# Four expert picks per tile moved out of the choice of experts and into the two output slots of the second layer

## The reference

```python
def second_block(x, c, ...):
    for layer in range(DEPTH):                        # 2 layers
        h = modulate(rmsnorm(x, ...), sh1, sc1)
        y = mlstm_mixer(h, ...) if layer < 1 else stick_breaking_mixer(h, k_sh, v_sh, ...)
        x = x + g1[:, None, :] * y                    # the output product ends in w_out
        h = modulate(rmsnorm(x, ...), sh2, sc2)
        x = x + g2[:, None, :] * peer_ffn(h, ...)

def peer_ffn(h, w_q, sub_keys, peer_u, peer_v):       # per block of 128 tokens
        q = einsum('td,de->te', xb, w_q)              # 8 heads
        s = einsum('thpk,pnk->thpn', q, sub_keys)
        s_top, i_top = lax.top_k(s, 16)
        ...                                           # 16 of 256 pairs -> expert numbers, softmax g
        u = jnp.take(peer_u, expert, axis=0)
        act = gelu(einsum('thkd,td->thk', u, xb))
        vv = jnp.take(peer_v, expert, axis=0)
        return einsum('thk,thkd->td', g * act, vv)
```

## Time and profile before

| | |
|---|---|
| Median of 3 runs | 2549.08 us (2549.06 to 2549.9) |
| Profiled execution | span 2555.0 us; no other time of it is given |
| PE busy | 81% of the span |
| DVE busy | 67% |
| DMA share, while experts are gathered | 0.9 or more in 21 of the last 22 slices |
| Gathers (software_dynamic queue) | 57.4% of 16 engines' span |

### The profile page before, as it was taken

How to read it: one execution, slowest core, us unless ns; L and a number is a source line. 1 busy time by engine, 2 the same in 40 slices (tenths; PEclk the granted TensorE clock), 3 DMA queues, 4 the chain that set the end, 5 groups by cost and what they waited for, 6 DMA issues and landing times.

```text
span 2555.0 us, 33871 instructions
## 1 busy us (share of the span) xinstructions
PE 2064.9 (81%) x12150; PEld 1390.3 (54%) x12150; DVE 1720.0 (67%) x3454; ACT 953.7 (37%) x2101; POOL 652.0 (26%) x631
## 2 busy tenths in 40 slices
PE   8999999999999999997755587795587787555555
PEld 7999898899989979874211132261133344111111
DVE  5687777768777767575985556538956745955444
ACT  4444443454444345432332225322325623222222
POOL 0000001000000100033454433324433424344443
PEclk9999999999999999998877798797798889677777
DMA  7545577664547754379999999999999989999998
GB/s 300 212 168 202 200 272 282 245 246 167 205 180 266 288 203 165 135 280 378 411 417 419 422 419 422 409 415 421 421 419 418 421 360 363 390 407 421 422 421 355
DMA packets 110515, 828.17 MB, mean 324 GB/s; under 512 B 14384, under 2 KB 15296, under 8 KB 30992
## 3 DMA queue, kind: packets, MB, share of 16 engines
q0 software_dynamic: 90000, 595.97, 57.4%
q1 hardware_dynamic: 20352, 230.08, 23.5%
HBM read 824.95 MB, written 1.05 MB: 323 GB/s over the span
## 4 chain that ended last, share of the span: by engine, by line
PE 48%; DMA 22%; DVE 16%; ACT 5%; issue 4%; DVEq 2%; POOL 1%; ACTq 1%; PEldq 0%; SPq 0%; POOLq 0%; PEld 0%
PE pd L600 14%; PE pa L600 11%; DMA ring_b<-in_peer_uv,eidx 10%; PE pr L1225 9%; DMA wring<-in_peer_uv,eidx 7%; PE pr L600 5%; DMA ring_c<-in_peer_uv,eidx 3%; DVE wring L2588 2%; DVE ring_b L2588 2%; PE pa L1246 2%; PE pa L1340 2%; DVE wring_r L1887 2%; PE pd L1246 1%; DMA aring<-in_ada_rows 1%; DMA wring<-in_w_mix 1%
## 5 line engine op out<-in xcount | busy, mean ns | idle before, releaser
L1225 PE MATMUL pr<-ring_b,junk 128*64 128x512 f32 x928 | 391.0, 789 | 171.2 <-ACT junk L1653 166.5
L1225 PE MATMUL pr<-wring,junk 128*64 128x512 f32 x888 | 366.4, 781 | 174.4 <-ACT junk L1653 172.2
L1831 POOL DMA_INDIRECT ring_b<-in_peer_uv,eidx x232 | 272.0, 1173 | 605.1 <-PE pr L1225 377.7
L2588 DVE CUSTOM_DVE_ANT_0 ring_b<-ring_b,hrow 128x1024 f32<-128x1024 f32 x232 | 282.9, 1225 | 211.0 <-DMA ring_b<-in_peer_uv,eidx 201.7
L2588 DVE CUSTOM_DVE_ANT_0 wring<-wring,hrow 128x1024 f32<-128x1024 f32 x222 | 270.2, 1224 | 189.5 <-DMA wring<-in_peer_uv,eidx 184.5
L1831 POOL DMA_INDIRECT wring<-in_peer_uv,eidx x222 | 251.0, 1131 | 317.9 <-PE pr L1225 271.5
L1643 ACT ACTIVATE gel<-dots 128x2 f32<-128x2 f32 x255 | 51.8, 203 | 699.5 <-DVE dots L2588 697.5
L1225 PEld LDWEIGHTS pr<-ring_b,junk 128*64 128x64 f32 x928 | 90.3, 167 | 392.4 <-ACT junk L1653 264.6
L1225 PEld LDWEIGHTS pr<-wring,junk 128*64 128x64 f32 x888 | 83.8, 164 | 385.0 <-ACT junk L1653 277.4
L1817 POOL DMA_DIRECT2D aring<-in_ada_rows x112 | 60.2, 538 | 841.7 <-DVE adal L1982 841.5
L1887 DVE TENSOR_TENSOR wring_r<-wring,wtop 128x2048 fp32r<-128x2048 f32 x76 | 171.8, 2262 | 56.4 <-ACT wtop L1370 54.2
(11 more groups left out here) (417 smaller groups left out, 4484.0 us busy)
## 6 DMA issues: line engine op xcount, KB each, us to landing
wring<-in_w_mix SPq DMA_DIRECT2D x38, 2048.0 KB, 8.5
aring<-in_ada_rows POOLq DMA_DIRECT2D x112, 512.0 KB, 5.2
wring<-in_w_stick SPq DMA_DIRECT2D x24, 2048.0 KB
wring<-in_w_ffn SPq DMA_DIRECT2D x22, 2048.0 KB, 8.3
wring<-in_w_lstm SPq DMA_DIRECT2D x12, 2048.0 KB, 7.7
wring<-in_w_back SPq DMA_DIRECT2D x8, 2048.0 KB, 8.2
wring<-in_w_back SPq DMA_DIRECT2D x4, 1536.0 KB, 7.2
ring_b<-in_peer_uv,eidx POOLq DMA_INDIRECT x232
```

What stands on the lines that cost most here:

```text
L1225: m = nc.tensor.matmul(pr[half][side, :], diag[:, p % DIAGS, :], row(p)[:, D + half * 512:D + (half + 1) * 512], start=p in FIRST_OF_SIDE, ...
L1831: pool.indirect_dma_start(out=row(q), out_offset=None, in_=ins["peer_uv"], in_offset=bass.IndirectOffsetOnAxis(ap=eidx[:, tt % NT, CHOSEN[ ...
L2588: m = nc.vector.tensor_tensor_reduce(out=row(q)[:, 0:D], in0=row(q)[:, 0:D], in1=hrow[:, q // PICKS % NT, SIDE[q], :], scale=1.0, scalar=0 ...
```

## The change

The plan gets a new entry, "mid", of four picks between "o" and the first output slot. The picks of the choice go from 41 to 37 for block 0 and from 31 to 27 for block 1. PE serves picks in the middle of each output slot (after four of its eight products): up to "mid" - 2 in slot 6 and up to "mid" in slot 7. DVE serves picks up to "mid" instead of "o" ahead of the first output product. ACT's calls read the same table; its next call after "o" already reaches past "mid". All picks from there to the end of the choice come four places earlier.

```diff
-    out, q, step = ((3, 3, 41), (2, 2, 31))[t]
+    out, q, step = ((3, 3, 37), (2, 2, 27))[t]
-                   + [("heads", 2)] + groups_of(t) + [("o", 2), ("out0", out), ("out1", out), ("fnorm", 2), ...
+                   + [("heads", 2)] + groups_of(t) + [("o", 2), ("mid", 4), ("out0", out), ("out1", out), ("fnorm", 2), ...
...
-            def tile_rows(bank, full, m, src):
+            def tile_rows(bank, full, m, src, halfway=lambda: None):
                 weights2(m)
                 b = bank()
                 for k in range(KC):
+                    if k == KC // 2:
+                        halfway()
                     i = nc.tensor.matmul(b[:, :], src(k), wring[:, m % R2, k, :], start=(k == 0), stop=(k == KC - 1))
...
                 for j in (6, 7):
-                    tile_rows(bank_d, pd_full, m0 + j, lambda k: hT[:, k, cut])
+                    tile_rows(bank_d, pd_full, m0 + j, lambda k: hT[:, k, cut],
+                              lambda j=j: weighted(tt, at["mid"] - (2 if j == 6 else 0), False))
...
-                picks(tt, at["o"])
+                picks(tt, at["mid"])
                 add_gated(t, 0, upto("out0", "out1"), stick_done)
```

More of the change, by code:

```diff
@@ L136, in plan_of @@
 def plan_of(t):
-    out, q, step = ((3, 3, 41), (2, 2, 31))[t]
+    out, q, step = ((3, 3, 37), (2, 2, 27))[t]
     return counted(0, [("first", 2), ("norm", 2), ("cols", 4), ("col0", 2), ("col1", 2)] + [(("in", j), 3) for j in range(6)]
-                   + [("heads", 2)] + groups_of(t) + [("o", 2), ("out0", out), ("out1", out), ("fnorm", 2), ("fcols", 2), ("fcol0", 1), ("fcol1", 1)]
+                   + [("heads", 2)] + groups_of(t) + [("o", 2), ("mid", 4), ("out0", out), ("out1", out), ("fnorm", 2), ("fcols", 2), ("fcol0", 1), ("fcol1", 1)]
                    + [(("q", j), q) for j in range(4)] + [("keys", 5)] + choice("choose", step, 2))
```

## The result

| | median | lowest to highest | runs |
|---|---|---|---|
| Before | 2549.06 us | 2544.4 to 2553.49 | 15 |
| Changed | 2555.88 us | 2551.18 to 2560.24 | 15 |

The ratio is 1.0026, with a 95% interval of 1.0018 to 1.0033: the changed kernel is 6.6 us slower by the ratio and 6.8 us by the medians. The forecast was +0.9 us. Single runs of one kernel lie up to 5 us from their median, so two single profiles can't be set against each other by their spans. The profiled pair shows it: the changed kernel's span is 2550.2 us, 4.8 us shorter than the 2555.0 us of the kernel before.

What follows compares the result with a forecast made beforehand. The gather stream was taken as the main bound, with DVE bounding the two choices of experts. Block 0's -0.1 us and block 1's +1.0 us gave +0.9 us, 2549.1 to 2550.0 us, range 2545.0 to 2555.5 us.

Steps and rivals of the forecast that it cites:

- Output slots: PE serves three pairs of picks inside the slots, so the second output product is ready 5.8 us later in each block.
- POOL's longest wait: Sign at block 1's output slots: POOL's idle time of 20.72 us falls to about 10 us.
- The rival by which the cut frees no place early: PE waits for diagonals in the cut and the hole stays; +5.8 us, chance 0.04.
- Block 0: Choice starts 8.2 us late and is 8.3 us shorter; sum -0.1 us, between -2.5 and +4.9 us.
- the filled hole of block 0: Stream at block 0's output slots: the 1.8 us lost at 346 GB/s is filled by the four added rows.
- the step that failed: Block 1's norm and query slots: delay between 5.8 and 7.8 us, taken as 6.8 us, so the choice starts 6.8 us late.
- Theory C: From the experiments: block 1's row 2.83, issued just ahead of two weight fetches, lands late; DVE waits about 5.5 us before the norm.
- The choice: Block 1's choice: four dots fewer, 5.1 us, and 0.7 us of waits, so 5.8 us shorter.
- Less than 5 us: Sign that the forecast is wrong: the choices are shorter by less than 5 us, or by more than 9.
- The slower rival: DVE in both choices gives back only its dots: 16.0 - 10.2 = +5.8 us, 2555 us; chance 0.12.
- the upper bound of 7.8 us: Delay of block 1's query slots if rows land at half rate while weights are fetched.
- seven rows at 2.49 us: Block 1's output slots: rows behind pick 2.73 are through some 14 us after it landed, near 2061.5, when the stream dries up.

Runs made afterwards that it cites:

- the second profile of the kernel before: The kernel before, run and profiled again without an edit; ratio 1.0000 to the kernel before, span 2546.0 us.
- its own control: The kernel before with block 1's fetches of the weights of slots 8 and 9 started behind the norm's transposes; ratio 1.0020 to the kernel before.

## Why the prediction was wrong

**Output slots: right.** The cut holds up the second product by 5.9 us in both blocks (block 0: 22.1 us for 16.2 from the first slot, block 1: 20.4 for 14.5), forecast 5.8; in the second profile of the kernel before block 0 took 17.5 us, which makes it 4.6. PE waits for no diagonal in the cut, and the stream's rate there is 428 to 431 GB/s. POOL's longest wait fell to 8.51 us, where about 10 was forecast (in the second profiles 16.29 us before and 5.72 us after). The rival by which the cut frees no place early is out.

**Block 0: right.** The first search began at 1738.6 us of the profile, not 1729.1, with the slots already 1.3 us later. First slot to first search 109.7 us (87.6 + 22.1) against 101.6 us (85.4 + 16.2): 8.1 us late, forecast 8.2. The choice is 6.4 us shorter (103.6 for 110.0), forecast 8.3, and the stretch from there to block 1's slots 2 to 3 us shorter, which wasn't forecast; the filled hole of block 0 (1.8 us) may be most of it, but no run separates this. Together that is about nothing, forecast -0.1, and the experiment on block 0 alone has 1.0007.

**Block 1: the step that failed** is "The norm's transposes and the query slots behind them need some of these rows, which now land with the fetch of a slot's weights beside them, so their delay lies between 5.8 and 7.8 us: 6.8 us". Measured are 10.2 us (90.6 for 80.4 with the block alone; 90.2 and 90.3 in two profiles of the changed kernel) and 15 us in one. Theory C holds. Before the change the two rows that the norm's dots need were there when the dots came, issued 8 us and more ahead of the first fetch (2045.7 and 2049.9, the fetch 2058.3). The four picks dealt into the slots used up this lead, and of the rows behind them 2.83 is issued 1.5 us ahead of the first of two fetches of 2 MB. It lands more than 20 us later, PE idles 8 to 9 us ahead of the transposes instead of 4.3, and the query slots start that much later. My step had two faults. It took the larger of two delays, PE's and the stream's, where they come one behind the other: the second product is 5.9 us late, and between it and the transposes another 5.5 us pass (16.2 for 10.7). And it had the row share the engines with the fetch of one slot, at half its rate at worst; the row lay behind both fetches, 9.9 us of transfer, with the gathers at a third of their rate. In the first profile of the changed kernel the row of 2.83 is waited for only 1.03 us and the search is as late, since the product was later there (slot 6 lost 1.7 us to the clock) and the next rows are waited for. That the fetches are the cause is shown from two sides: made small, the loss goes (0.9999 for 1.0024); made late, it goes against its own control. That the waits for rows come with the deal and not with the cut is shown by the two halves: without the cut DVE waits for three rows, with the cut alone for none ahead of the norm. Why the changed kernel with small fetches is 3.4 us slower by stages and not by the ratio stays open.

The choice then gave back 4.4 us of the 5.8 forecast (92.9 for 97.3 us with the block alone; 4.2 to 5.5 us in the three profiles of the changed kernel). Less than 5 us was among the signs that the forecast is wrong. Tile 3 went on at 421 GB/s as before, from the finish of tile 2 to the end 316.6 to 318.6 us in every profile. The sum by stages is 10.2 - 4.4 = +5.8 us; the ratios say 6 to 9.

**The slower rival** gave nearly the time (+5.8 us) but not the mechanism. It wanted both choices more than 15 us late in sum; they were 8.1 + 10.2 = 18.3 us late. It has block 0 lose 3.1 us of this (8.2 - 5.1), where nothing is lost that the runs can tell, and it knows of no row behind the fetches. Its chance of 0.12 was too small, since it rested on bounds for the late rows of block 1 that were too narrow.

**The Trainium skill.** I had weighed its rule that each DMA engine takes turns between the queue of the gathers and that of plain transfers (DMA: Bandwidth & Descriptors, section "SWDGE vs HWDGE vs iDMA"), and had it set the upper bound of 7.8 us. The trace agrees that they take turns, 127 packets for 125; what I made of it, half the rate, does not hold, since a packet of the fetch carries twice as much: the gathers fell from 421 to 129 GB/s, a third. On cutting a row of products (TensorE: Matmul & The Clock Gate, section "HAM oscillation — how this bites in real kernels") the trace agrees so far that a cut without waits did no harm: there were none, and the slots' halves take 3.70 us at full clock. No run has a wait in the cut.

**What misled.** The one profile that I had was of an execution above nearly all others in length, with 2.97 us lost to the clock in the very slot that the change touches. From block 1's first slot to the first search it took 87.6 us, the second profile 80.4, so that beside it the changed kernel's 90.2 us look like a small loss. And POOL's idle time at the slots was 20.72 us there, 16.29 us in the second profile, which made the hole look longer than it is in other runs. One of my sums is also off: seven rows at 2.49 us are 17.4 us, not the 14 us by which I had the stream run dry near 2061.5. The trace has it run dry there all the same (303 GB/s from 2060 to 2061, then 107), so the place was right, but not by that sum.

## What to carry to other kernels

- The mean rate of a stream tells when one row is there only if everything is counted that is served ahead of it, and here this took in two fetches issued after it on another queue. For a step that waits for a single transfer, look at what is issued within a few us of it on the other queues, how large their packets are, and how far ahead of its use the row had landed: this lead is what a change of order spends.
- A stretch of a stream that looks like a hole can be a transfer of another queue running alone. Filling it makes the two compete.
- Filling a hole in a stream that is thought to be the bound brings nothing if the work that fills it pushes the next serial step (here sum, norm, transposes, query slots) past it; where the stage behind gives back only the dots that it lost, the difference stays.
- Work that is dealt elsewhere is waited for elsewhere: the two picks moved behind the norm came back ahead of the choice.

## What was not expected of the hardware

The row of 2.83 took 22.3 us from issue to dot beside two such fetches, and at most 17.1 us (2076.39 - 2059.34) with these cut to an eighth. The row of a merged timeline that names both fetches (x2, 9.76 us) runs from the first issue to the second, 0.33 us each, and is no time of transfer.

The changed kernel's first query slot took 7.41 us or, in one profile, 9.45 us. Such differences of the clock may be a part of why single runs of one kernel spread by up to 5 us to either side.
